# Attention by pairs of heads, a new order at the end of the first feed forward, and more places for unsplit weight blocks, in a fused two-block kernel

## What is computed

```
x = first_block(x, c, ctx, ...)     # the stage of the change, cut:
  mod = silu(c) @ w_ada + b_ada                        # 6 x 1024 values
  q, k, v, u = split(modulate(rms_norm(x)) @ w_in)     # 8 heads of 64
  s = [q_rot k_rot^T * scale + bias (256 keys), q k_ctx^T * scale (256 keys)]
  attn = softmax(s) @ [v; v_ctx]
  conv = silu(layer_norm(depthwise_conv31(glu(u))))
  x += g1 * (concat(attn, conv) @ w_out)
  x += g2 * relu(modulate(rms_norm(x)) @ w_mlp1)^2 @ w_mlp2
x = rms_norm(x)
x = second_block(x, ...)            # two attentions, gates, gated feed forward
```

## Time and profile before

| | us |
|---|---|
| median of 3 runs | 814.83 (814.05 to 815.26) |
| the profiled execution, whole | 814.35 |
| its span | 812.5 |
| TensorE, VectorE, ScalarE, GpSimd busy in the span | 758.4, 494.1, 393.1, 20.0 |
| first attention, 123.2 to 203.8 | 80.6 |
| output product to `up1(0, 1)`, 203.8 to 246.3 | 42.5 |
| last `up1(7, 0)` to the end of `down1(7, 1)`, 388.9 to 421.5 | 32.6 |
| from there to `qa(0)`, 421.5 to 459.4 | 37.9 |

### The profile page before, as it was taken

The page is one execution under the profiler, slowest core; times in us unless marked ns, Lnnn a source line. Parts: engine busy times, 40 slices in busy tenths (PEclk is TensorE's granted clock), DMA queues, the critical chain, the costliest instruction groups (busy, mean ns, idle before and its releaser), DMA issues.

```text
span 812.5 us, 9467 instructions
## 1 busy us (share of the span) xinstructions
PE 758.4 (93%) x3696; PEld 596.7 (73%) x3696; DVE 494.1 (61%) x892; ACT 393.1 (48%) x664; POOL 20.0 (2%) x39
## 2 busy tenths in 40 slices
PE   4799998997989999999986999999999999999996
PEld 0578875664768888888775877777787888888875
DVE  1579978863565444454557789975575645545443
ACT  1375226583356445445435546666545534434431
POOL 1020000100000000000000000000000000000000
PEclk9899999997999999999998999999999999999999
DMA  9794418964055545555171844334436754666411
GB/s 342 269 392 151 156 55 316 319 217 156 15 219 206 188 164 170 204 203 170 45 227 46 310 143 169 104 105 165 147 104 206 241 173 160 216 194 205 158 53 52
DMA packets 77756, 144.88 MB, mean 178 GB/s; under 512 B 4032, under 2 KB 27584, under 8 KB 77712
## 3 DMA queue, kind: packets, MB, share of 16 engines
q1 hardware_dynamic: 75776, 138.19, 49.7%
q0 software_dynamic: 1520, 5.03, 1.8%
q10 hardware_dynamic: 416, 1.06, 0.3%
HBM read 143.22 MB, written 1.05 MB: 178 GB/s over the span
## 4 chain that ended last, share of the span: by engine, by line
PE 80%; DVE 8%; ACT 5%; DMA 4%; issue 3%; POOL 0%; SPq 0%; DVEq 0%; POOLq 0%; ACTq 0%
PE bank L381 23%; PE bank L382 22%; PE bank L383 22%; PE bank L363 5%; DVE WL L1314 4%; DMA W<-in_w_ada 2%; PE bank L398 2%; PE bank L524 1%; ACT WH L884 1%; PE bank L504 1%; PE bank L736 1%; PE bank L758 1%; DVE X L1318 1%; DMA W<-in_w_mlp 1%; DMA W<-in_w_in 1%
## 5 line engine op out<-in xcount | busy, mean ns | idle before, releaser
L1314 DVE TENSOR_TENSOR WL<-W,WH 128x1024 fp32r<-128x1024 f32 (+1 forms) x214 | 247.8, 1208 | 67.7 <-ACT WH L884 66.7
L381 PE MATMUL bank<-WH,AH 128*128 128x512 f32 (+1 forms) x608 | 243.9, 401 | 13.6 <-DVE WL L1314 7.3
L382 PE MATMUL bank<-WL,AH 128*128 128x512 f32 (+1 forms) x608 | 237.5, 391 | 0.0
L383 PE MATMUL bank<-WH,AL 128*128 128x512 f32 (+1 forms) x608 | 237.2, 390 | 0.0
L884 ACT ACTIVATE WH<-W 128x1024 fp32r<-128x1024 f32 (+1 forms) x214 | 210.1, 1041 | 14.2 <-DMA W<-in_w_in 4.9
L381 PEld LDWEIGHTS bank<-WH,AH 128*128 128x128 f32 x608 | 116.0, 191 | 43.4 <-issue 13.0
L383 PEld LDWEIGHTS bank<-WH,AL 128*128 128x128 f32 x608 | 115.8, 190 | 24.4
L382 PEld LDWEIGHTS bank<-WL,AH 128*128 128x128 f32 x608 | 116.1, 191 | 22.3 <-issue 0.5
L381 PE MATMUL bank<-WH,HH 128*128 128x512 f32 x216 | 84.8, 393 | 5.1 <-DVE HL L1565 5.1
L383 PE MATMUL bank<-WH,HL 128*128 128x512 f32 x216 | 84.2, 390 | 0.0
L382 PE MATMUL bank<-WL,HH 128*128 128x512 f32 x216 | 84.1, 389 | 0.0
(11 more groups left out here) (233 smaller groups left out, 723.1 us busy)
## 6 DMA issues: line engine op xcount, KB each, us to landing
W<-in_w_mlp SPq DMA_DIRECT2D x32, 1024.0 KB, 5.4
W<-in_w_in SPq DMA_DIRECT2D x28, 1024.0 KB, 6.9
W<-in_w_ada SPq DMA_DIRECT2D x24, 1024.0 KB, 7.0
W<-in_w_gate SPq DMA_DIRECT2D x22, 512.0 KB, 4.1
W<-in_w_up SPq DMA_DIRECT2D x22, 512.0 KB, 5.1
W<-in_w_down SPq DMA_DIRECT2D x11, 1024.0 KB, 4.9
W<-in_w_out SPq DMA_DIRECT2D x8, 1024.0 KB, 5.1
bias<-in_rpb POOLq DMA_DIRECT2D x8, 256.0 KB, 8.0
```

The lines of the kernel that those rows point to most:

```text
L381: e.matmul(po, hs, wh[:, k, c0:c0 + cw], start=first and k == 0, stop=False)
L382: e.matmul(po, hs, wl[:, k, c0:c0 + cw], start=False, stop=False)
L383: ins = e.matmul(po, ls, wh[:, k, c0:c0 + cw], start=False, stop=last and k == unit.nk - 1)
L1314: e.tensor_tensor(m.WL[unit.slot][:, c], m.W32[unit.slot][:, c], m.WH[unit.slot][:, c].bitcast(F32), ALU.subtract).then_inc(S["w_lo"], 1)
```

## The change

Attention runs over u = 0 to 7, a pair of heads (2i, 2i + 1) and a token half. The two heads' scores use the upper and lower 64 rows of the array and a bank each; the output of `pv1` comes out turned, two heads side by side in 64 columns each, with V as the stationary operand. One reduction over 512 columns (the bias tile is padded with 256 zero columns that GpSimd fills) gives the maximum, one exponential follows, and probabilities are divided by their sum before the transposes (`norm1`). O1 and its transposes go, `rows2` has one buffer in place of two; `out1` takes the attention half first. The convolution has 18 more taps ahead of the loop, its root becomes a power of 128 x 256 on GpSimd (ScalarE only scales and adds), and its Silu and rounding follow the loop. Unsplit blocks may also lie in a slot's high-part place (`WX`, slots 12 to 15), with semaphores of their own. At the end of the first feed forward `up1(7, 1)` comes ahead of both `down1` pairs; `between` loses two scalar steps and one wait, and its low parts are spread over its waits; `first2` computes qb ahead of s. In both feed forwards `norm_turn` for half 1 moves into the middle of the product behind it.

```
+    def out(i):
+        add("out", "w_out", 0 if i > 1 else 4, 4, [("w_out", 512 * (i % 2), 512)], True, ("out_mm", OUT_AT[i, 1]))
...
+    for n in range(16):
...
+        add(("ada2", i), "w_ada", 4 * half, 4, [("w_ada", c0, 512)], False, ("ada2_mm", n + 1))
+        if n == 7:
+            out(0)
+            out(1)
+        if n == 11:
+            out(2)
+            out(3)
...
-    slots += [2, 3, 4, 0, 5, 2, 3, 1, 4, 5, 2, 3, 4, 5, 2, 4, 5, 2, 5, 2]
+    slots += [2, 12, 3, 13, 4, 14, 5, 15, 0, 1, 2, 12, 3, 13, 4, 5, 2, 12, 3, 13]
...
-        slots.append((5, 2, 0, 1, 3, 4)[(len(slots) - 38) % 6])
...
+        slots.append((2, 3, 0, 1, 4, 5)[(len(slots) - 38) % 6])
...
     for unit, slot in zip(units, slots):
-        unit.slot, unit.old = slot, last[slot]
...
+        places = [slot, slot + 10] if unit.split else [slot]
+        unit.old = [last[p] for p in places if p in last]
...
     def bias(h):
         if h >= 4:
-            w.wait_ge(S["max1"], 3 * (2 * (h - 4) + 1) + 2)
+            w.wait_ge(S["max1"], 4 * (h // 2 - 2) + 3 + h % 2)
+        elif h > 1:
+            w.wait_ge(S["qk_turned"], 8)
         else:
             w.wait_ge(S["kx"], 4)
-        e.dma_start(m.bias[h % 4][:, :, :], d["rpb"][h].rearrange("(t p) n -> p t n", p=128)).then_inc(S[f"l_b{h % 4}"], 16)
+        if h < 4:
+            e.memset(m.bias[h][:, :, 256:512], 0.0).then_inc(S["bias_zero"], 1)
+        e.dma_start(m.bias[h % 4][:, :, 0:256], d["rpb"][h].rearrange("(t p) n -> p t n", p=128)).then_inc(S[f"l_b{h % 4}"], 16)
...
+    w.wait_ge(S["eps"], 2)
+    w.wait_ge(S["conv_act"], 2)
+    e.tensor_tensor(m.crs[:, :], m.crs[:, :], m.stat[:, 94:95].to_broadcast([128, 256]), ALU.pow).then_inc(S["conv_rs"], 1)
...
-    def product(us, H, L, tb, bk, sem, ready, cw=512):
+    def product(us, H, L, tb, bk, sem, ready, cw=512, between=None):
         for i, unit in enumerate(us):
+            if between and i:
+                between()
             part(unit, H, L, unit.nk * i, tb, bk, i == 0, i == len(us) - 1, sem, ready, 0, cw)
...
+    def scores1(u):
...
+        i, tb = u // 2, u % 2
+        banks = SCORE1_BANKS[tb]
         w.wait_ge(S["qk_act"], 8)
...
+        take(banks[0])
+        take(banks[1])
+        for q, k, c0 in ((m.qrT, m.kT, 0), (m.qT, m.kcT, 256)):
+            for j in range(2):
+                r = slice(64 * j, 64 * j + 64)
+                ins = e.matmul(bank[banks[j]][:, c0:c0 + 256], q[r, i, tb * 128:tb * 128 + 128], k[r, i, :], start=True, stop=True)
+                if c0:
+                    ins.then_inc(S["scores1"], 1)
+        for j in range(2):
+            frees(banks[j], ("max1", 2 * u + j + 1))
...
-        w.wait_ge(S["exp1"], 2 * n + 2)
+        w.wait_ge(S["p1_norm"], n + 1)
         b = turn(four(m.P1[n % 2]), "p1_turned")
-        frees(b, PT1_AT[n])
...
-    def pv1(n):
...
+        frees(b, ("pt1", n + 1))
+    def pv1(u):
...
+        w.wait_ge(S["pt1"], 2 * u + 2)
...
-        if h == 0:
-            take(2 + tb)
+        take(5)
         for i in range(4):
-            ins = e.matmul(bank[2 + tb][:, hc], m.PT1[n % 3][:, i * 128:i * 128 + 128],
-                           (m.V if i < 2 else m.VC)[:, i % 2, hc], start=i == 0, stop=i == 3)
+            for j in range(2):
+                h = u // 2 * 2 + j
+                ins = e.matmul(bank[5][64 * j:64 * j + 64, 0:128], (m.V if i < 2 else m.VC)[:, i % 2, h * 64:h * 64 + 64],
+                               m.PT1[j][:, i * 128:i * 128 + 128], start=i == 0, stop=i == 3, tile_position=(0, 64 * j))
         ins.then_inc(S["pv1"], 1)
+        frees(5, ("o1_lo", u + 1))
...
-        mod_unit(by["ada2", i][half], 4 * half, 4 + i % 2, "ada2_mm")
+        mod_unit(by["ada2", i][half], 4 * half, 4, "ada2_mm")
         if half:
-            frees(4 + i % 2, ("rows2", i + 1))
-        elif i:
-            mod_second_tail(i - 1)
+            frees(4, ("rows2", i + 1))
...
+    for u in range(8):
+        if u < 7:
+            scores1(u + 1)
+        mod_second(2 * u)
+        if u:
+            mod_second_tail(u - 1)
+            pv1(u - 1)
+        if u < 7:
+            mod_second(2 * u + 1)
+        turn1(2 * u)
+        turn1(2 * u + 1)
+        if u == 4:
             conv_sum(m.cacc, "conv", 124, ("conv_dve", 4))
-        if n == 10:
+        if u == 5:
             conv_sum(m.csq, "conv_act", 1, ("conv_act", 2))
-        if n > 1:
-            pv1(n - 2)
-        turn1(n)
-    pv1(14)
-    pv1(15)
-    frees(2, ("o1", 1))
-    frees(3, ("o1", 2))
+    mod_second(15)
+    pv1(7)
...
         k0, n = ((4, 0), (4, 1), (0, 0), (0, 1))[i]
-        ready = ("k_conv", 1) if k0 else ("o1_lo", tb + 1)
-        part(by["out"][i], m.AH, m.AL, k0, tb, 2 * n + tb, k0 == 4, k0 == 0, "out_mm", lambda k: ready)
-        if k0 == 0:
+        part(by["out"][i], m.AH, m.AL, k0, tb, 2 * n + tb, k0 == 0, k0 == 4, "out_mm",
+             lambda k: ("k_conv", 1) if k0 else ("o1_lo", 2 * k + tb + 1))
+        if k0:
...
+    for it in OUT_ORDER[:7]:
+        out1(*it)
+    norm_turn(0, 0)
     out1(1, 1)
...
+    up1(1, 0, 0, lambda: norm_turn(1, 1))
...
     up1(7, 0)
+    up1(7, 1)
+    hid_turn1(7, 0)
     down1(6, 0, False, False)
-    hid_turn1(7, 0)
+    hid_turn1(7, 1)
     down1(7, 0, False, True)
-    up1(7, 1)
     down1(6, 1, False, False)
-    hid_turn1(7, 1)
     down1(7, 1, False, True, lambda: norm_turn(2, 0))
...
-        product(by["s"], m.AH, m.AL, tb, 2 + tb, "s_mm", n_ready(1, tb), 200)
-        frees(2 + tb, ("p2_out", 3 * tb + 2))
+        product(by["qb"], m.AH, m.AL, tb, tb, "p2_mm", n_ready(1, tb))
+        frees(tb, ("p2_out", 3 * tb + 2))
         if tb == 0:
             norm_turn(3, 1)
-        product(by["qb"], m.AH, m.AL, tb, tb, "p2_mm", n_ready(1, tb))
-        frees(tb, ("p2_out", 3 * tb + 3))
+        product(by["s"], m.AH, m.AL, tb, 2 + tb, "s_mm", n_ready(1, tb), 200)
+        frees(2 + tb, ("p2_out", 3 * tb + 3))
...
+    up2(1, 0, 0, lambda: norm_turn(5, 1))
...
+    def exp1(n):
...
+        w.wait_ge(S["max1"], n + 1)
         if n > 1:
             w.wait_ge(S["p1_turned"], n - 1)
...
+        e.activation(m.P1[n % 2][:, :], m.s1[n % 4][:, :], ACT.Exp, bias=m.mneg[:, n:n + 1], scale=-1.0,
+                     accum_out=m.lsum[:, n:n + 1]).then_inc(S["exp1"], 1)
...
+    def turned1_out(n):
...
+        copy(m.PT1[n % 2][:, :], bank[m.turn_bank["p1_turned", n + 1]][:, :], "pt1")
...
+    def o1_hi(u):
...
+        w.wait_ge(S["pv1"], u + 1)
+        copy(m.AH[:, i, tb * 128:tb * 128 + 128], bank[5][:, 0:128], "o1_hi")
...
+    for u in range(8):
+        exp1(2 * u)
+        exp1(2 * u + 1)
+        if u:
+            o1_hi(u - 1)
+        if u in (1, 2, 4, 5):
+            hi()
+        if u == 7:
+            turned1_out(14)
+            turned1_out(15)
+        w.wait_ge(S["ada2_mm"], 2 * u + 2)
+        w.wait_ge(S["qr"], 2)
+        if u:
+            w.wait_ge(S["rows2_turned"], u)
+        copy(m.rows2[:, :], bank[4][:, :], "rows2")
+        if u < 7:
+            turned1_out(2 * u)
+            turned1_out(2 * u + 1)
+        if u == 4:
             w.wait_ge(S["conv_dve"], 4)
             e.activation(m.csq[:, :, :], m.ccen[:, :, :], ACT.Square).then_inc(S["conv_act"], 1)
-        if n == 10:
+        if u == 5:
             w.wait_ge(S["conv_sums"], 2)
-            e.activation(m.crs[:, :], bank[m.turn_bank["conv_sums", 2]][:, 0:256], ACT.Sqrt, bias=m.stat[:, 95:96],
+            e.activation(m.crs[:, :], bank[m.turn_bank["conv_sums", 2]][:, 0:256], ACT.Identity, bias=m.stat[:, 95:96],
                          scale=1.0 / 512).then_inc(S["conv_act"], 1)
...
+    o1_hi(7)
+    w.wait_ge(S["conv_dve"], 5)
+    for c in range(4):
+        e.activation(m.cacc[:, c, :], m.ccen[:, c, :], ACT.Silu, bias=m.lnb[:, c:c + 1],
+                     scale=m.lng[:, c:c + 1]).then_inc(S["conv_act"], 1)
...
+    copy(m.AH[:, 4:8, :].rearrange("p a b -> p (a b)"), m.cacc[:, :, :].rearrange("p a b -> p (a b)"), "conv_act")
...
+    hi()
+    relu_sq(7, 1)
+    hid_hi1(7, 0)
+    hi()
+    hid_hi1(7, 1)
     hi(2)
...
+            hi(mid)
+        w.wait_ge(S["rstd"], 8 + 2 * tb)
+        copy(m.S1[:, tb, 512:1024], m.X[:, tb, 512:1024], "nscale_act", m.stat[:, 47 + 2 * tb:48 + 2 * tb])
+    between(0, 0)
...
-    between(1, lambda: hi(2))
+    between(1, 1)
...
-    hi()
...
-    taps(44)
...
+        e.tensor_tensor_reduce(out=m.s1[n % 4][:, :], in0=m.bias[h % 4][:, tb, :], in1=bank[SCORE1_BANKS[tb][j]][:, :], scale=-1.0,
+                               scalar=-SENT, op0=ALU.add, op1=ALU.min, accum_out=m.mneg[:, n:n + 1]).then_inc(S["max1"], 1)
+    def norm1(u):
+        w.wait_ge(S["exp1"], 2 * u + 2)
+        e.reciprocal(m.rl[:, 2 * u:2 * u + 2], m.lsum[:, 2 * u:2 * u + 2]).then_inc(S["rl1"], 1)
+        w.wait_ge(S["rl1"], u + 1)
+        for n in (2 * u, 2 * u + 1):
+            times(m.P1[n % 2][:, :], m.P1[n % 2][:, :], m.rl[:, n:n + 1], "p1_norm")
...
+    def o1_lo(u):
...
```

(98 more changed lines are left out.)

233 lines of the change are left out of this document (68 added, 165 removed).

## The result

The changed kernel takes 818.46 us (median of 6 runs, 818.04 to 819.18) against 814.83 (814.05 to 816.76, 6 runs): ratio 1.0043, 95% interval 1.003 to 1.0056, slower by 0.4% where 790 was forecast. The profiled execution has a span of 816.5 us against 812.5.

What follows compares the result with a forecast made beforehand. TensorE, busy 93% of the span, was taken as the bound. Terms -15.4 + 1 - 3.2 - 6.3 - 0.9 = -24.8 took the span from 812.5 to 787.7, forecast 790 us, range 779 to 802.

Steps and rivals of the forecast that it cites:

- the price of the power: Convolution's root on GpSimd, 256 columns: 8 us taken, between 0.8 and 100, costing 2 us after 6 hidden.
- Rival (a): Slow GpSimd power: from 6 us on each delays everything; 12 to 32 us has chance 0.10, over 32 0.06.
- Attention: Attention stage: 80.6 us becomes 65.2, a gain of 15.4, between -10 and -21.
- rival (c): Attention's head pairs don't overlap: a u takes 8.1 us, the stage 71 to 74, kernel 798; chance 0.07.
- the turns that are VectorE's: Attention loop: two turns where VectorE's list sets the pace, about 2 us over TensorE's each.
- Output stage: Stage after the attention: fewer transposes and waits but a late m1[1] load; +1 us, between -3 and +4.
- Rival (d): Output stage: the late m1[1] load costs more and the clock falls; +5 us, 795; chance 0.12.
- End of the feed forward: Last turn of the first feed forward: two waits for hid's low part go, 32.6 becomes 29.4, -3.2 us.
- From there to `qa(0)`: The 37.9 us after the feed forward's last turn: waits for low parts shrink, -6.3 us, between -2 and -9.
- Second feed forward: Second feed forward: the wait of 0.91 gets half a product ahead of it, -0.9 us.
- Rival (e): Attention loop: bias lands late and VectorE's list, not TensorE's, is the pace in all u; 797; chance 0.08.
- Rival (b): GpSimd and VectorE exclude each other during the power, so 8 us cost 5; kernel 793; chance 0.12.

Runs made afterwards that it cites:

- e7: Changed kernel with the power done for 64 of the 256 columns only, the root left out for the other 192: 786.53 us.
- e1: Changed kernel with the convolution's root again Sqrt on ScalarE and a reciprocal on VectorE, no power on GpSimd: 784.18 us.
- e5: e1 with the slot rotation changed so block m1[1] waits for the attention half of the output product: 777.29 us.
- e11: e5 with conv_scale moved behind the last division and block qi's low halves spread over the waits of between(0): 774.70 us.
- e9: e5 with the order qi, s, qb turned back in the loads and on three engines, low parts still spread: 778.78 us, one run.
- e10: e5 with the low parts of between(1) in one piece behind the residual, order qi, qb, s kept: 781.38 us, one run.
- e2: e1 with five powers of various sizes and a multiplication added on GpSimd in the first feed forward: 783.68 us, one run.

## Why the prediction was wrong

**The step that failed is the price of the power.** "Most of that 0.4 is set-up, I think ... I take 8": the 0.4 between a fill and a one-column power was read as almost all fixed cost. Measured, 0.4 of the 0.56 is fixed and 0.16 is per column, and 0.16 times 256 is 41. That most of it is fixed was right, but 8 us for 256 columns leaves only 0.03 per column, a fifth of what it is, and nothing in the row spoke for so little. The point above which the sign turns, 0.12 us per column, lay well inside what was open (0.8 to 100 us). The chance of 0.06 for over 32 us leaned on the argument that two operands are costly to set up, for which no row spoke. The estimate from the Trainium skill (GPSIMD Engine Reference, 3.1 Elementwise), 0.6 to 2.6 us here, was further off; the trace agrees with it for the multiplication (0.61) and not for the power.

**Rival (a) is what happened**, by its own formula: the power is free for 6 us (measured 6.7), each further one costs one (e7), and the sign turns at 32 us. At 41.2 it gives 790 - 2 + 35 = 823. It was 818.5, because the rest was better than forecast.

**The other terms**, with the power out of the sum (788), against e1, whose root costs VectorE 1.75 and ScalarE two tables:

- Attention: 63.2 forecast without the power, 59.04 measured. Scores and pv at 1.1 measured 1.06 and 1.02, a u 6.08 for 6.3, so rival (c) falls. TensorE's own work was 52.4 for 54.2. The excess was 6.6 us in waits and none at the lower clock, for 9 assumed, and it was made up otherwise: 1.3 for the first pair (2.5 assumed), 0.9 for the turns that are VectorE's (4), 2.2 ahead of the two sums (1), 2.24 behind `conv_scale`. The -21.5 lies at the stated low end, -21, but not for its reason: by the prediction's own 54.2, no excess at all would be -26. That the number came out at that end is partly luck.
- Output stage: +1 forecast, -0.4 measured. The late load of `m1[1]` cost its 4 (4.25), in the place named and with ScalarE's list between it and TensorE, and e5 shows that the slot alone did it. Rival (d), five more, did not come; the rest of the stage was better by one.
- End of the feed forward: -3.2 forecast, -2.2 measured. The two waits for `hid` went, one of 1.16 ahead of `norm_turn(2, 0)` came: the `lo(2)` ahead of `between(0)`, which was charged to qi as "up to 1", delays the norm and not qi (e11).
- From there to `qa(0)`: -6.3 forecast, -7.3 measured, but not for the reason named. That was the cover from qb; with the low parts spread, the order is worth nothing (e9), the spreading itself 1.8 (e10), and the rest is not traced to one edit.
- Second feed forward: -0.9, as forecast.
- Rival (e) falls: VectorE was TensorE's limit in two turns (waits of 0.73 and 0.18), not in all, and no reduction waited for a bias load.
- Rival (b), the lock, falls: VectorE's low parts began in the middle of powers of 21 and 41 us and took 1.16 and 2.35, as without them. The Trainium skill (SBUF — State Buffer, "SBUF: two separate sides") states that a VectorE instruction with two inputs in SBUF and a GpSimd instruction that reads SBUF lock each other out for the whole instruction. The low part (W - high) beside the power is such a pair, and the measured times differ from that rule; the measurement decides.

So a forecast of 788 for the change without its power would have been 4 too slow (784.18). The error of 28 is one term that was 32 too small, less these 4. The range has a slip of its own: the low ends of the parts (-21, -3, -3.2, -9, -0.9) add up to 778, not 779.

## What to carry to other kernels

Where the price of an operation is open over a factor of a hundred and the trace has it on one column only, the whole forecast hangs on that price. A one-column row gives a fixed part and a slope together, and here a slope of 0.12 us per column was enough to turn 25 us of gain into a loss. Run the operation at two widths first: e2 did that beside other work and was no slower than e1 (783.68 against 784.18, one run). The reciprocal root of 256 columns was far cheaper as a square root on ScalarE and a reciprocal on VectorE (1.75 us, and two table loads of 1.28) than as a power on GpSimd (41); for one column the power takes 0.56. And the waits in a chain of small steps are a place for weight low parts, one by one: this turned a wait of 2.60 into four short ones of 1.5 in all (e10 against e5) and took away one of 1.15 (e11).

## What the runs showed of the hardware

- GpSimd's power takes the same time on 32 and on 128 partitions (21.48 and 21.15 us for 128 columns) and 67 times as long as a multiplication (41.2 against 0.61 us for 256 columns).
- The same wait did not always have the same effect on TensorE's clock, in single profiled executions. Behind a wait of 2.24 us, with the same work ahead of it, the last 35 matmuls of the attention ran at 2.4 GHz in e1 and for the most part at 1.2 GHz in e5, 1.6 us longer. In e9 and e10 matmuls behind that wait were slow too, in e2 not; what decided it stays open. Busy time of that stretch, the clock in the third column from the right, in e1:

```profile
179.17:182.77 3.60, 3.60 (x34) 2.18 (x35) 0.83 (x5) 2.11 (x5) 0.00 (x0) 1.00 0.09 22
```

and in e5:

```profile
180.28:185.46 5.18, 5.18 (x35) 2.77 (x35) 0.83 (x5) 2.21 (x5) 0.00 (x0) 0.67 0.10 21
```
